# Dense V tiles loaded in pairs: two buffers of two tiles in place of four buffers of one

## The chip, the cores and the metric

The kernel runs on one core of a Trainium2 chip. The metric is the device time of one execution in microseconds (us), the median of several executions. Trace times count from the first instruction of one profiled execution.

## What is computed

One layer of a hybrid backbone for 256 tokens of width 2048: a long-convolution branch and a state-space branch, merged and projected, and then a retrieval of experts (PEER). Only the last step of the retrieval matters here. For each token there are 128 chosen experts (8 heads, 16 each) out of 16,384, and their rows of `peer_v` (2048 wide) are added up with weights:

```python
def block(args):
    hb, ib, gb = args
    act = jax.nn.gelu(jnp.einsum('td,tkd->tk', hb, p['peer_u'][ib]))
    return jnp.einsum('tk,tkd->td', act * gb, p['peer_v'][ib])
```

After it comes the last layer norm of `alpha * h + gate * ffn`, and the output.

## The kernel before

`block_ef` holds the end of the kernel. The sum over `peer_v` is done in two ways at once, one for each half of the 2048 columns.

**Columns 0 to 1023, dense, on TensorE.** All 16,384 rows of `peer_v` are read as 128 tiles (`v_dense[i]`, 128 experts x 1024 columns, float32, 512 KB, 4 KB for each partition). The weights were spread out beforehand into matrices `W[t][...]` (most of them zero) by one-hot products, which keep DVE and TensorE at work until the sums can begin. `sum_tile(i)` (L2716 to L2726) waits for tile i and multiplies it for both token tiles t and both column halves k into the four PSUM banks `2 * t + k`, where all 128 tiles are added up. The trace has two matmul records for each of these float32 products, eight for a tile. The last product of a tile raises `vt_used`.

**The buffers.** `v_tile` (L1968) is `m.yhy`, cut into four slots of 1024 columns. The two rows `h2` of modulated tokens, which the dot products with `peer_u` read, lie in the same memory: row 0 in slots 0 and 1, row 1 in slots 2 and 3. So tiles 0 and 1 wait until the first half of those dot products is done, and tiles 2 and 3 until all are. From tile 4 on, the load of tile i waits for `vt_used` to reach i - 3, that is, until tile i - 4 has been multiplied. SP (SyncE) issues them in order (L2122 to L2129), and nothing else goes through SP meanwhile; after them come the four stores of the output.

**Columns 1024 to 2047, gathered, on GpSimd and DVE.** For each of the 2 x 128 pairs (token tile, chosen expert), GpSimd issues a gather (L2165) of 128 rows of 1024 columns, again 512 KB in rows of 4 KB, and DVE adds it, times a coefficient, to `acc` (`add_row`, L2498; the first two are L2495). Eight slots hold gathered rows: four in `scores`, four in `m.h`. GpSimd waits with gather k until the row that was in its slot has been added. The last 24 gathers (from `V_LATE` = 232) use only the four slots of `scores`, because `m.h` is loaded again with the residual rows (ACT, L2303) once 232 rows are added.

**The end.** When all 256 rows are added, DVE finishes the late columns (`finish_late_columns`, L2506 to L2513), then reads the four PSUM banks of the dense sums (`finish_early_columns`, from L2521; it waits for `ffn_pe`), normalises, and SP stores the output. DVE reads the banks in the order in which TensorE's last tile finishes them.

So two chains run side by side, and both draw on the same 16 DMA engines: load, multiply, release of a `v_tile` slot (SP, TensorE); and gather, add, release of a row slot (GpSimd, DVE).

Of the kernel before, what the change touches and what calls it, by code (L numbers as in the profile page):

```python
# [41 lines left out]
PH, NKEY, TOPK = 8, 128, 16  # L42
# [1852 lines left out]
def block_ef(nc, m, d):  # L1895
# [4 lines left out]
    with ExitStack() as ctx:  # L1900
# [3 lines left out]
        def sem(name):  # L1904
            return ctx.enter_context(nc.semaphore(name))
# [62 lines left out]
        v_tile = m.yhy[:].rearrange("p a b -> p (a b)").rearrange("p (s n) -> p s n", n=HALF_D)  # L1968
        NVT = 4
# [50 lines left out]
        w_a = sem("expert_weights_copied")  # L2020
        v_in = [sem(f"v_row_{n}_gathered") for n in range(NV)]
        acc_v = sem("v_rows_added")
        vt_in = [sem(f"v_tile_{n}_loaded") for n in range(NVT)]
        vt_used = sem("v_tiles_done")
        ffn_pe = sem("ffn_summed")
        gt2_in = sem("last_gate_row_loaded")
# [14 lines left out]
        def dve_rows(j):  # L2041

            return j + 1 - min((j + 1) // 4, N_PE)
# [50 lines left out]
        with nc.Block() as block:  # L2094

            @block.sync
            def _(sp):
                for dst, src in ((sc2, d.mod_rows[2 * KT:3 * KT]), (sh2, d.mod_rows[KT:2 * KT])):
                    sp.dma_start(dst.rearrange("p (o n) -> p o n", o=1),
                                 src.rearrange("(o a) n -> o (a n)", o=1).unsqueeze(0).to_broadcast([P, 1, D])).then_inc(mods_in, 16)  # L2100
                sp.dma_start(iota[:], d.iota).then_inc(small, 16)

                def store_h(t):
                    sp.wait_ge(h_fin, t + 1)
                    sp.dma_start(d.h_rows[:, t, :], m.h[:, t, :]).then_inc(h_st[t], 16)

                for n in range(RING + OUT_EARLY, N_OUT + SQ_TILES - N_HOME):
                    sp.wait_ge(m.w_used, START_OUT + n - RING + 1)
                    src = d.w_out[OUT_ORDER[n]] if n < N_OUT else d.w_q[n - N_OUT + (N_HOME if n >= N_OUT + 4 else 0)]
                    sp.dma_start(m.ring[:, n % RING, :], src).then_inc(m.w_full[n % RING], 16)  # L2110
                    if n == 26:
                        store_h(0)
                    if n == N_OUT:
                        sp.dma_start(keys[:].rearrange("p a b -> p (a b)"), d.keys.rearrange("p a b c -> p (a b c)")).then_inc(keys_in, 16)
                    if n == N_OUT + 3:
                        for k, home in enumerate(homes):
                            if k == 2:
                                store_h(1)
                                sp.wait_ge(h2_p, 2 * TT + 1)
                            sp.dma_start(home, d.w_q[4 + k]).then_inc(home_in[k], 16)  # L2120

                for i in range(NKEY):  # L2122
                    if i == 0:
                        sp.wait_ge(dot_v, dve_rows(ROWS // 2 - 1))
                    if i == 2:
                        sp.wait_ge(dot_v, N_DVE)
                    if i >= NVT:
                        sp.wait_ge(vt_used, i - NVT + 1)
                    sp.dma_start(v_tile[:, i % NVT, :], d.v_dense[i]).then_inc(vt_in[i % NVT], 16)  # L2129

                for k in range(2 * TT):
                    sp.wait_ge(out_v, k + 1)
                    t, part = k // 2, slice(k % 2 * HALF_D, (k % 2 + 1) * HALF_D)
                    sp.dma_start(d.out[t * P:(t + 1) * P, part], m.h[:, t, part]).then_inc(out_st, 16)
                sp.wait_ge(out_st, 16 * 2 * TT)
# [174 lines left out]
            def _(v):  # L2310
# [177 lines left out]
                def add_row(k):  # L2488

                    t, first = k % TT, k < TT  # L2490
                    _, landed = v_before(k)
                    coefficient = gate[:, v_pair(k):v_pair(k) + 1]
                    v.wait_ge(v_in[v_at(k)], landed)
                    if first:
                        nc.vector.tensor_scalar(acc[:, t, :], v_slot[v_at(k)], coefficient, None, ALU.mult).then_inc(acc_v, 1)  # L2495
                    else:
                        v.wait_ge(acc_v, k - 1)
                        nc.vector.scalar_tensor_tensor(acc[:, t, :], v_slot[v_at(k)], coefficient, acc[:, t, :],  # L2498
                                                       ALU.mult, ALU.add).then_inc(acc_v, 1)
# [93 lines left out]
            def _(pe):  # L2593
# [121 lines left out]

                def sum_tile(i):  # L2716

                    pe.wait_ge(vt_in[i % NVT], 16 * (i // NVT) + 16)
                    for t in range(TT):
                        for k in range(2):  # L2720
                            mm = nc.tensor.matmul(ps[:, 2 * t + k, :], W[t][i // HALF][:, i % HALF, :], v_tile[:, i % NVT, k * CH:(k + 1) * CH],
                                                  start=(i == 0), stop=(i == NKEY - 1))
                            if i == NKEY - 1:
                                mm.then_inc(ffn_pe, 1)
                    if i < NKEY - 1:
                        mm.then_inc(vt_used, 1)  # L2726
# [19 lines left out]
                for u in range(UNITS):  # L2746
                    for h in range(NB):
                        k = NB * u + h
# [18 lines left out]
                for i in range(NKEY):  # L2767
                    sum_tile(i)
# [16 lines left out]
def build(nc, d):  # L2785
    with ExitStack() as ctx:
# [36 lines left out]
        m.b_in = ctx.enter_context(nc.semaphore("e_bias_row_loaded"))  # L2823
        block_d(nc, m, d)
        block_ef(nc, m, d)


# [116 lines left out]
```

## Time and profile before

| | us |
|---|---|
| median of 3 runs (3486.7 to 3492.4) | 3490.19 |
| the profiled execution | 3493.18 |
| its span, first to last instruction | 3491.5 |
| first and last record of a dense sum, TensorE | 2966.4, 3405.6 |
| last addition of a gathered row begins, DVE | 3459.65 |
| DVE begins to read the dense sums | 3468.26 |

The times in the rows are read as positions in the span: the first eight tenths of it do other work, the stretch from 2966 to 3461 is the two chains, and the last 30 us are the finish. PE is TensorE, PEld its weight loads, DVE is VectorE, POOL is GpSimd and SP is SyncE. DMA queue q0 carries the gathers that GpSimd issues, q1 what SP issues (in this stretch the dense tiles alone), q10 what ACT issues. A packet of this stretch is one row of 4 KB, so a dense tile is 128 packets, to which 16 small ones are added that report its end: 144.

### The profile page before, as it was taken

How to read it: one execution, taken by the hardware profiler on the slowest of the kernel's cores; microseconds unless marked ns; L12 is line 12 of the kernel's file. 1: busy time of each engine (PE TensorE's matmuls, PEld its weight loads, DVE VectorE, ACT ScalarE, POOL GpSimd, SP SyncE). 2: the span in 40 equal slices, each digit the busy share in tenths (PEclk: the TensorE clock that was granted, in tenths of full speed). 3: DMA queues.
4: the chain of work that ended last, by engine and by line, in shares of the span. 5: the costliest groups of instructions: out<-in, count | busy, mean ns of one | idle time of the engine just before them, and what ended most of it. 6: DMA issues, size and time to landing. Idle time of an engine off the chain costs nothing. (4 is left out here: it accounts for less than half of the span.)

```text
span 3491.5 us, 35993 instructions
## 1 busy us (share of the span) xinstructions
PE 3175.9 (91%) x12602; PEld 2031.3 (58%) x12602; DVE 2136.3 (61%) x3994; ACT 635.7 (18%) x1127; POOL 996.9 (29%) x618
## 2 busy tenths in 40 slices
PE   7999999999999999999999999887677768999990
PEld 2456667575757666777544444666666766444440
DVE  6543444444434444665756425888899988666667
ACT  2312212121212122111000011233233424000000
POOL 0011102020211113000000011455644462876773
PEclk8999999999999999999999999998888889999995
DMA  9754454545364544554554597999998893999996
GB/s 359 291 219 181 181 200 166 216 152 224 129 234 154 209 183 182 202 186 174 206 180 169 211 334 281 384 374 377 394 385 337 318 396 152 394 419 420 419 419 245
DMA packets 171354, 930.26 MB, mean 266 GB/s; under 512 B 19736, under 2 KB 32857, under 8 KB 89305
## 3 DMA queue, kind: packets, MB, share of 16 engines
q1 hardware_dynamic: 85386, 494.13, 38.0%
q0 software_dynamic: 73728, 402.69, 28.9%
q10 hardware_dynamic: 12112, 31.79, 2.3%
q8 instruction: 74, 1.21, 0.1%
q14 instruction: 54, 0.44, 0.0%
HBM read 907.29 MB, written 21.23 MB: 266 GB/s over the span
## 5 line engine op out<-in xcount | busy, mean ns | idle before, releaser
L1078 PE MATMUL ps<-mT,ring 128*128 128x256 f32 (+1 forms) x4096 | 1168.9, 446 | 1.1 <-PEq L215 1.1
L1078 PEld LDWEIGHTS ps<-mT,ring 128*128 128x128 f32 x4096 | 774.9, 190 | 388.1 <-issue 318.3
L2156 POOL DMA_INDIRECT u_rows<-in_peer_u_dram,expert_indices x172 | 267.9, 1558 | 283.9 <-DVE dots L2453 117.0
L2453 DVE CUSTOM_DVE_ANT_0 u_rows<-u_rows,yhy 128x2048 f32<-128x2048 f32 x130 | 293.8, 2287 | 57.8 <-DMA u_rows<-in_peer_u_dram,expert_indices 44.6
L2669 PE MATMUL ps<-mT,turned_rows 128*128 128x128 f32 x2016 | 301.0, 304 | 22.3 <-ACT turned_rows L2230 20.7
L2669 PEld LDWEIGHTS ps<-mT,turned_rows 128*128 128x128 f32 x2016 | 279.1, 216 | 38.0 <-issue 38.0
L710 POOL TENSOR_TENSOR dd<-mask_f,dt_g 128x1024 f32<-128x1024 f32 x16 | 30.4, 1897 | 933.1 <-DVE dt_g L980 932.4
L2165 POOL DMA_INDIRECT scores<-in_v_rest_dram,expert_indices x140 | 203.1, 1451 | 136.0 <-DVE turned_rows L2495 56.2
L870 DVE SCALAR_TENSOR_TENSOR conv<-ps,tap_g,conv 128x510 f32<-128x510 f32 (+1 forms) x48 | 33.8, 704 | 338.7 <-ACT conv L731 338.7
L2498 DVE SCALAR_TENSOR_TENSOR turned_rows<-scores,expert_gate,turned_rows 128x1024 f32<-128x1024 f32 x138 | 176.9, 1286 | 96.8 <-DMA scores<-in_v_rest_dram,expert_indices 95.8
L2230 ACT COPY turned_rows<-ps 128x512 f32<-128x512 f32 x252 | 144.1, 586 | 439.7 <-PE ps L2661 433.6
L2661 PE MATMUL ps<-ident,u_rows 128*128 128x128 f32 x672 | 117.2, 318 | 84.6 <-DMA u_rows<-in_peer_u_dram,expert_indices 84.6
L2498 DVE SCALAR_TENSOR_TENSOR turned_rows<-h_rows,expert_gate,turned_rows 128x1024 f32<-128x1024 f32 x116 | 148.7, 1286 | 72.7 <-DMA h_rows<-in_v_rest_dram,expert_indices 72.6
L2165 POOL DMA_INDIRECT h_rows<-in_v_rest_dram,expert_indices x116 | 166.2, 1433 | 57.0 <-issue 29.3
L2156 POOL DMA_INDIRECT h_rows<-in_peer_u_dram,expert_indices x84 | 133.4, 1588 | 116.2 <-DVE dots L2453 55.3
L2453 DVE CUSTOM_DVE_ANT_0 h_rows<-h_rows,yhy 128x2048 f32<-128x2048 f32 x63 | 142.9, 2287 | 29.2 <-DMA h_rows<-in_peer_u_dram,expert_indices 22.6
L884 DVE SCALAR_TENSOR_TENSOR ada_sums<-ada_tiles,csil,ada_sums 128x1024 f32<-128x1024 f32 x120 | 153.9, 1283 | 4.0
L2661 PEld LDWEIGHTS ps<-ident,u_rows 128*128 128x128 f32 x672 | 94.8, 166 | 96.7 <-DMA u_rows<-in_peer_u_dram,expert_indices 93.5
L870 DVE SCALAR_TENSOR_TENSOR hyb<-ps,tap_g,hyb 128x255 f32<-128x255 f32 x48 | 23.1, 480 | 199.0 <-ACT hyb L731 199.0
L1245 PE MATMUL ps<-ring,mT 128*128 128x256 f32 x512 | 129.1, 386 | 0.3 <-PEq L645 0.3
L731 ACT ACTIVATE conv<-ps,tap_g 128x512 f32<-128x512 f32 (+1 forms) x48 | 35.5, 742 | 510.2 <-PE ps L1078 509.1
L2713 PE MATMUL ps<-keys 128*128 128x128 f32 x512 | 105.5, 335 | 21.9 <-DVE keys L2477 19.8
(392 smaller groups left out, 4475.2 us busy)
## 6 DMA issues: line engine op xcount, KB each, us to landing
ring<-in_w_stream_dram SPq DMA_DIRECT2D x160, 1024.0 KB, 4.9
ada_tiles<-in_w_ada_dram SPq DMA_DIRECT2D x64, 1024.0 KB, 6.7
yhy<-in_v_dense_dram SPq DMA_DIRECT2D x128, 512.0 KB
ring<-in_w_mix_dram SPq DMA_DIRECT2D x48, 1024.0 KB, 4.8
ring<-in_w_mod_dram SPq DMA_DIRECT2D x32, 1024.0 KB, 10.5
ring<-in_w_out_dram SPq DMA_DIRECT2D x32, 1024.0 KB, 7.3
rows<-cum_rows_scratch SPq DMA_DIRECT2D x16, 1536.0 KB, 13.0
ring<-in_w_q_dram SPq DMA_DIRECT2D x12, 1024.0 KB, 9.4
```

What stands on the lines that cost most here:

```text
L870: nc.vector.scalar_tensor_tensor(view[:, :, 1:T], src[:, :, 0:T - 1], tap[:, ci, 0:1], view[:, :, 1:T], ALU.mult, ALU.add).then_inc(conv_v, 1)
L884: nc.vector.scalar_tensor_tensor(adas[:], adat[:, b, j, :], m.csil[:, k, 0:1], adas[:], ALU.mult, ALU.add).then_inc(ada_used, 1)
L1078: mm = nc.tensor.matmul(ps[:, k % 4, 0:n], m.ring[:, slot, kt * P:(kt + 1) * P], m.mT[:, kt, 0:n], start=(kt == 0), stop=(kt == KT - 1))
L1245: mm = nc.tensor.matmul(gate_region(m, j), a, w, start=(i == 0 and kk == 0 and j == 6), stop=(i == 3 and kk == 1 and j in (1, 3, 5, 6)))
L2156: nc.gpsimd.indirect_dma_start(u_slot[j % NU], None, d.peer_u, bass.IndirectOffsetOnAxis(ap=eidx[:, j:j + 1], axis=0)).then_inc(u_in[j % N ...
L2165: nc.gpsimd.indirect_dma_start(v_slot[v_at(k)], None, d.v_rest, bass.IndirectOffsetOnAxis(ap=eidx[:, v_pair(k):v_pair(k) + 1], axis=0)).th ...
L2230: nc.scalar.copy(turned_rows[:, g, :], ps[:, g % 2, :]).then_inc(turn_a, 1)
L2453: nc.vector.tensor_tensor_reduce(out=u_slot[j % NU], in0=u_slot[j % NU], in1=h2[:, t, :], scale=1.0, scalar=0.0, op0=ALU.mult, op1=ALU.add ...
L2498: nc.vector.scalar_tensor_tensor(acc[:, t, :], v_slot[v_at(k)], coefficient, acc[:, t, :], ALU.mult, ALU.add).then_inc(acc_v, 1)
L2661: mm = nc.tensor.transpose(ps[:, g % 2, a * P:(a + 1) * P], row[:, i * P:(i + 1) * P], m.ident[:])
L2669: mm = nc.tensor.matmul(ps[:, 2 + k % 2, 0:P], turned_rows[:, g, a * P:(a + 1) * P], m.mT[:, i, T + t * P:T + (t + 1) * P], start=(i == 0) ...
L2713: mm = nc.tensor.matmul(ps[:, 4 + k % 4, a * NKEY:(a + 1) * NKEY], one_hot[:, s, :], one_hot[:, s + 1, :], start=True, stop=True)
```

## The change

Two tiles are loaded by one DMA of 1 MB. Pair k (tiles 2k and 2k + 1) goes to slots 0 and 1 if k is even, and 2 and 3 if it is odd. `sum_tile` is the same apart from its wait: both tiles of a pair wait for the pair's semaphore, so the first tile waits until both have landed. A pair's load waits until both tiles of pair k - 2 have been multiplied. The memory used is the same.

```diff
-        vt_in = [sem(f"v_tile_{n}_loaded") for n in range(NVT)]
+        vt_in = [sem(f"v_tile_pair_{n}_loaded") for n in range(2)]
...
-                for i in range(NKEY):
-                    if i == 0:
+                for k in range(NKEY // 2):
+                    if k == 0:
                         sp.wait_ge(dot_v, dve_rows(ROWS // 2 - 1))
-                    if i == 2:
+                    if k == 1:
                         sp.wait_ge(dot_v, N_DVE)
-                    if i >= NVT:
-                        sp.wait_ge(vt_used, i - NVT + 1)
-                    sp.dma_start(v_tile[:, i % NVT, :], d.v_dense[i]).then_inc(vt_in[i % NVT], 16)
+                    if k >= 2:
+                        sp.wait_ge(vt_used, 2 * (k - 1))
+                    sp.dma_start(v_tile[:, 2 * (k % 2):2 * (k % 2) + 2, :],
+                                 d.v_dense[2 * k:2 * k + 2].rearrange("a p n -> p a n")).then_inc(vt_in[k % 2], 16)
...
-                    pe.wait_ge(vt_in[i % NVT], 16 * (i // NVT) + 16)
+                    pe.wait_ge(vt_in[i // 2 % 2], 16 * (i // NVT) + 16)
```

The order of the instructions on SP, from the last load before the dense tiles to the end. `yhy` is the memory of `v_tile`. The semaphores have names of earlier stages, whose numbers are used again. Before:

```order
L2110 DMA ring<-in_w_q_dram 128x2048 [waits ring_tiles_used] x8
L2129 DMA yhy<-in_v_dense_dram 128x1024 [waits filter_abs_summed]
L2129 DMA yhy<-in_v_dense_dram 128x1024
L2129 DMA yhy<-in_v_dense_dram 128x1024 [waits filter_abs_summed]
L2129 DMA yhy<-in_v_dense_dram 128x1024
L2129 DMA yhy<-in_v_dense_dram 128x1024 [waits b_dve_step] x124
L2134 DMA out_dram<-h_rows 128x1024 [waits ada_tile_0_loaded] x4
```

and now:

```order
L2110 DMA ring<-in_w_q_dram 128x2048 [waits ring_tiles_used] x8
L2129 DMA yhy<-in_v_dense_dram 128x2x1024 [waits filter_abs_summed] x2
L2129 DMA yhy<-in_v_dense_dram 128x2x1024 [waits small_loaded] x62
L2135 DMA out_dram<-h_rows 128x1024 [waits ada_tile_0_loaded] x4
```

128 loads become 64 of twice the size. The first two have the waits that tiles 0 and 2 had, and the other 62 wait for the products, `vt_used`.

On TensorE, four of the last tiles. A row with a wait is the first product of a tile, and the semaphore it names is that of the tile's load. Before:

```order
L2721 MATMUL ps<-yhy,ring 128x512 [waits x_loaded]
L2721 MATMUL ps<-yhy,ring 128x512
L2721 MATMUL ps<-yhy,mT 128x512 x2
L2721 MATMUL ps<-yhy,ring 128x512 [waits dft_matrix_loaded]
L2721 MATMUL ps<-yhy,ring 128x512
L2721 MATMUL ps<-yhy,mT 128x512 x2
L2721 MATMUL ps<-yhy,ring 128x512 [waits small_loaded]
L2721 MATMUL ps<-yhy,ring 128x512
L2721 MATMUL ps<-yhy,mT 128x512 x2
L2721 MATMUL ps<-yhy,ring 128x512 [waits first_small_loaded]
```

and now:

```order
L2722 MATMUL ps<-yhy,ring 128x512 [waits x_loaded]
L2722 MATMUL ps<-yhy,ring 128x512
L2722 MATMUL ps<-yhy,mT 128x512 x2
L2722 MATMUL ps<-yhy,ring 128x512 [waits x_loaded]
L2722 MATMUL ps<-yhy,ring 128x512
L2722 MATMUL ps<-yhy,mT 128x512 x2
L2722 MATMUL ps<-yhy,ring 128x512 [waits dft_matrix_loaded]
L2722 MATMUL ps<-yhy,ring 128x512
L2722 MATMUL ps<-yhy,mT 128x512 x2
L2722 MATMUL ps<-yhy,ring 128x512 [waits dft_matrix_loaded]
```

No product has moved. Four semaphores in turn have become two, each waited for by two tiles in a row, of which the second finds it raised already.

## Rows read from the trace of the kernel before

**Rows 1.** By stage: busy us (instructions) of PE, PEld, DVE, ACT, POOL; clock, DMA share, GB/s

```profile
2950.00:3000.00 50.00, 48.41 (x146) 24.92 (x147) 37.37 (x85) 9.52 (x19) 28.60 (x18) 1.00 0.59 234
3200.00:3250.00 50.00, 50.00 (x118) 22.23 (x117) 32.84 (x26) 0.00 (x0) 36.46 (x26) 1.00 1.03 420
3350.00:3400.00 50.00, 50.00 (x117) 22.04 (x116) 32.58 (x27) 0.00 (x0) 37.48 (x26) 1.00 1.03 420
3400.00:3450.00 50.00, 6.17 (x15) 2.47 (x13) 36.12 (x29) 0.00 (x0) 28.50 (x27) 0.59 0.90 332
```

**Rows 2.** The dense sums' line L2721: duration ns min/median/max, first and last start

```profile
L2721 PE MATMUL ps<-yhy,gates x256: 592/592/697, 2966.4 to 3184.1; 128*128 128x512 f32 x128
L2721 PE MATMUL ps<-yhy,mT x256: 592/592/593, 3188.0 to 3405.6; 128*128 128x512 f32 x128
```

**Rows 3.** DVE at the end, in order of time: start us, us

```profile
3459.65 1.28 DVE L2498 SCALAR_TENSOR_TENSOR turned_rows<-scores,expert_gate,turned_rows 128x1024 f32<-128x1024 f32 x1 [1.13 <-DMA scores<-in_v_rest_dram,expert_indices]
...
3468.26 0.69 DVE L2521 TENSOR_TENSOR turned_rows<-keys,ps 128x512 f32<-128x512 f32 x1
```

**Rows 4.** Additions of gathered rows (L2498) alone, by stretch

```profile
3000.00:3400.00 400.00, 260.26 (x203) 1.00 1.03 420
3400.00:3414.00 14.00, 13.07 (x11) 0.81 1.02 414
3414.00:3461.00 47.00, 30.73 (x25) 0.50 0.80 279
```

**Rows 5.** GpSimd's gathers (L2165): duration ns min/median/max, first and last start

```profile
L2165 POOL DMA_INDIRECT scores<-in_v_rest_dram,expert_indices x136: 934/1491/7846, 2966.2 to 3454.2; - x136
```

**Rows 6.** SP's issues of dense tiles, in order of time

```profile
2970.17 0.33 SPq L2129 DMA_DIRECT2D yhy<-in_v_dense_dram  x1
...
3196.77 0.33 SPq L2129 DMA_DIRECT2D yhy<-in_v_dense_dram  x1
...
3392.47 0.33 SPq L2129 DMA_DIRECT2D yhy<-in_v_dense_dram  x1
```

**Rows 7.** DMA queues from 3395.15 to 3395.85: packets, MB, share of 16 engines

```profile
q0 software_dynamic: 79, 0.28, 98.8%
q8 instruction: 1, 0.02, 8.5%
```

**Rows 8.** DMA queues from 3199.30 to 3199.95, then from 3199.95 to 3202.60

```profile
q0 software_dynamic: 73, 0.27, 101.5%
q1 hardware_dynamic: 5, 0.00, 0.4%
...
q0 software_dynamic: 161, 0.59, 54.0%
q1 hardware_dynamic: 131, 0.52, 48.1%
```

**Rows 9.** Loads of 1 MB on q1 beside gathers of peer_u: L2110 from 2213 to 2272

```profile
L2110 SPq DMA_DIRECT2D ring<-in_w_q_dram x4: 328/328/328, 2213.5 to 2271.4; - x4
...
DMA to landing us min/median/max: 8.7/9.4/10.2
```

**Rows 10.** DMA queues from 2971.1 to 2973.5, where no gather moves

```profile
DMA packets 144, 0.52 MB, mean 218 GB/s; under 512 B 16, under 2 KB 16, under 8 KB 144
...
q1 hardware_dynamic: 144, 0.52, 62.8%
```

**Rows 11.** Short stretches with idle time on TensorE, each with the next one

```profile
2395.00:2398.40 3.40, 1.23 (x9) 1.03 (x10) 3.40 (x5) 0.87 (x2) 3.09 (x2) 1.00 0.99 371
2398.40:2401.80 3.40, 3.40 (x17) 3.40 (x18) 0.14 (x2) 0.79 (x2) 2.61 (x3) 0.50 1.05 388
...
2077.60:2081.00 3.40, 2.24 (x14) 1.35 (x12) 2.07 (x3) 2.16 (x7) 0.00 (x0) 1.00 0.99 265
2081.00:2084.40 3.40, 2.66 (x10) 1.45 (x10) 0.00 (x0) 3.40 (x11) 1.80 (x1) 1.00 1.01 429
```

## Prediction, before the changed kernel was run

> **What bounds the kernel now.** I read first the busy time by stage, then who waits at the end. From 3000 to 3400 two things are full: TensorE is busy 50 of every 50 us, and the DMA engines move 420 GB/s [rows 1]. After 3400 TensorE is done (its last record starts at 3405.6 [rows 2]), and what is left are gathered rows: the last addition begins at 3459.65, and DVE turns to the dense sums at 3468.26 [rows 3]. So the gathers set the end and the dense sums have slack: 3468.3 less some 3406 is 62 us, and a little more, since DVE reads four banks one after the other.
>
> TensorE's pace is (3405.6 - 2966.4) / 128 = 3.43 us for a tile [rows 2], so the dense tiles draw 0.524 MB / 3.43 us = 153 GB/s. The gathers take what is left, 267 GB/s: 203 rows in 400 us, 1.97 us for a row [rows 4]. An addition takes 1.28 us (260.26 / 203) and GpSimd can issue a gather in 0.93 us [rows 4, 5], so neither of them is the limit; the shared DMA bandwidth is. **Each byte that the dense tiles do not draw goes to the gathers.** That is why a slower TensorE need not be a loss here, up to the 62 us.
>
> **How long a load takes.** The question is whether a pair lands in time. Now: the last tile is issued at 3392.47 [rows 6], and up to 3395.85 no packet of q1 moves [rows 7]: it starts 3.4 us after its issue. In mid-stretch the tile issued at 3196.77 [rows 6] moves between 3199.95 and 3202.60, 0.52 MB in at most 2.65 us, with 161 gather packets beside its own 131 [rows 8]: the two queues share about evenly, and the start is 3.2 us behind the issue. With 0.5 us until the report is seen (my estimate, no row shows it), a tile lands 6.5 us after its issue. It has three tiles of time, 10.3 less 0.3 for the release, so 3.5 us are to spare; TensorE's full busy time agrees.
>
> **The change, part by part.** (1) *64 issues fewer on SP.* SP does nothing else, 0.33 us each [rows 6], hidden: nothing. The 16 small packets of each saved load are too short to count: five took 0.4% of the engines in 0.65 us [rows 8]. (2) *First pairs.* Pairs 0 and 1 have the waits of tiles 0 and 2 and land before 2966 as they did: nothing. (3) *The second tile's wait* finds its semaphore raised: nothing. (4) *The pair's load.* It is issued when pair k - 2 is done and needed when pair k - 1 is: 6.87 us later, less 0.3. It moves twice the bytes. Its start is not shown for a DMA of this shape; I keep 3.4 us. Two packets for one of before, at the same even share, take 4.7 to 5.1 us; with 0.5 us at the end it lands **9.0 us** after its issue. Lower bound: if it moved alone at 420 GB/s, 2.5 us, it would land at 6.4 and TensorE would not wait. Upper bound: loads of the same 1 MB on the same queue beside gathers took 8.7 to 10.2 us, median 9.4 [rows 9]. I take 9.0, by the packets, near that median.
>
> (5) *What TensorE waits.* With two buffers, pair k ends no earlier than pair k - 2 ends + 0.3 + 9.0 + 0.05 + 6.87 = 16.2 us later: two pairs in 16.2 us where it was 13.74. That is a wait of 2.4 us for every two pairs, in one piece or in two of 1.2; on average a pair takes **8.1 us** instead of 6.87. As first order, 62 pairs x 1.2 = 75 us, over the slack of 62. Two things change it.
>
> (6) *The gathers gain.* The dense draw falls to 1.05 MB / 8.1 = 130 GB/s, and the gathers get 290: 1.81 us for a row, 0.16 less. About 220 rows fall into this: 35 us. The 232nd row, added at about 3414 now (25 additions are in the last stretch, which starts at 3414 [rows 4]), comes at about 3380. The last 24 rows have four slots and take 47 us [rows 4]; now dense loads run beside them, so I give them 47 to 60, take 54, and the gathers end near 3434, 27 us earlier. TensorE by then has done 2 pairs (to 2980) and 454 / 8.1 = 56 more; the 6 that are left no longer share the bandwidth (a tile without gathers moved at 218 GB/s within 3.3 us of its issue [rows 6, 10], so 1 MB in 4.8 us and about 6 in all is in time) and take 41 us. TensorE ends at about 3475 instead of 3407.
>
> (7) *The end.* DVE's finish from the first read of a bank is 3491.5 - 3468.3 = 23.2 us [rows 3]; it can start 2.6 us before TensorE's end. 3475 + 20.6 = **3496**, 4 us above the span of before: the gathers' gain is spent, and TensorE ends last.
>
> (8) *The clock.* Where TensorE was busy 1.23 of 3.4 us, the next 3.4 us have a granted clock of 0.50, the lower level of 1.2 GHz; where it was busy 2.24 of 3.4 it stayed at 1.00 [rows 11]. A wait of 2.4 us in one piece leaves TensorE some 1.0 of 3.4 us, as in the first case; one of 1.2 us leaves 2.2, as in the second. A stretch at half clock costs 1.7 us of products. Between none of some 28 double periods (0) and two thirds of them (32 us), I take a third, 16 us. It is on the path now, since TensorE ends last. Sum: 3496 + 16 = 3512 of span; the executions lie 1.7 above the span in the profiled one, whose time is 3.0 above the median, so 1.3 less than that span: **3511**.
>
> **A rule weighed.** A tile issued at 2970.17, when no gather moves, is over by 2973.5, at 218 GB/s [rows 6, 10]; beside gathers it takes 6.5 us. The Trainium skill, "DMA: Bandwidth & Descriptors", section "Bandwidth", asks for DMAs of at least 1 MiB, and in "Anatomy of one DMA" prices one at 2.0 us plus its bytes at 436 GB/s. By that, an estimate for the pair is 4.4 us, inside the 6.6 that it has; the 6.5 us for half as much beside gathers disagree with it, and I go by the trace. It would make rival A true.
>
> **Rivals.**
> *A. Nothing waits* (the pair is in time, or the change only halves the number of issues). The draw is the same, and so is the time: 3490. It needs a landing within 6.6 us, which a single tile takes already beside gathers. It speaks for it that the tile has 3.5 us to spare; against it that the pair has 3.4 us less time and 2.4 us more to move.
> *B. TensorE waits, but less than its slack: faster.* Landing near 8 us: (8.0 + 7.2) / 2 = 7.6 us for a pair, a draw of 138 GB/s, 282 for the gathers, 0.1 us less for each of 220 rows, 24 us earlier at row 232, of which the last 24 rows give back some 10; TensorE ends near 3450 and the gathers set the end: 14 us off, 3476. It would follow if a pair moved in 3.8 us, two packets of its own for one of the gathers'. The skill's same page, "Queues, rings and completion order", says that an engine drains a whole packet of descriptors (9 to 17) of one queue before it turns to the next, which would favour the longer load so. Against it, the even mix through a tile's 2.6 us [rows 8]. The turn from faster to slower is at a landing of about 8.8 us without any loss of clock.
> *C. TensorE waits for more and the clock falls often: slower by more.* The forecast's own mechanism; its far end is a landing of 9.6 or more (start or movement longer for a DMA with two rows for each partition) and two thirds of the waits at half clock: (9.6 + 7.2) / 2 = 8.4 us, TensorE near 3488 + 32, 3541 of span.
> *D. The total bandwidth changes* because the packets of a pair alternate between two tiles 512 KB apart. 1% of 420 GB/s over 430 us is 4 us either way; no row shows it.
>
> **Chances.** Landing over 8.8 us and TensorE last, the forecast with its far end: 0.64 slower. Around the turning point (0.11) or rival A (0.05): 0.16 within. Rival B: 0.20. A measurement of this kernel tells about 0.2% (7 us) from no change, which is the bound of these three. The range takes in B and most of C, 3476 to 3540.
>
> **What the new profile would show.** TensorE's waits for the dense loads: 60 to 75 us in total, as pieces of up to 2.4 us (A: none; B: 30 to 45). The last record of the dense sums near 3480 to 3500, behind the last gathered row, which should be near 3425 to 3440. In mid-stretch DVE adds a row every 1.8 us, and q1 shows runs of 256 packets over about 5 us, starting 3.4 us after the issue. Granted clocks below 1.00 between 2980 and 3440. If the gathers still end last, B or A holds; if the pair's landing is below 8, step 4 is wrong; if TensorE waits as said and the clock stays at 1.00, step 8 is.

## The result: 0.8% slower, and TensorE ends last

The changed kernel takes 3515.6 us (median; 3511.6 to 3526.4) where the kernel before takes 3489.3 in the same comparison: a ratio of 1.008, 95% interval 1.0056 to 1.0104. 3511 was forecast, with 3476 to 3540 as the range.

The profiled execution is the longest of its four, 3526.4 us with a span of 3524.7, 11 us over the median. Terms read from its trace are therefore a little large; a second profile of the same kernel, below, lies at the median. In all the profiles of this document the first dense product starts between 2962.0 and 2968.5 us, though no edit changes the work ahead of it. Where two profiles differ by a few us, the lengths of the chains say more than the times at which they end.

The stages, columns as in [rows 1]:

```profile
3100.00:3150.00 50.00, 44.26 (x101) 18.57 (x101) 36.02 (x29) 0.00 (x0) 30.18 (x29) 1.00 1.03 420
3200.00:3250.00 50.00, 43.49 (x96) 18.20 (x94) 35.37 (x29) 0.00 (x0) 31.22 (x29) 0.97 1.03 420
3350.00:3400.00 50.00, 39.31 (x77) 16.74 (x78) 31.61 (x25) 0.00 (x0) 24.34 (x22) 0.86 0.99 400
3450.00:3500.00 50.00, 50.00 (x118) 22.09 (x117) 0.00 (x0) 0.00 (x0) 0.00 (x0) 1.00 0.41 147
```

TensorE is no longer full between 3000 and 3400: in the second row it is busy 43.5 of 50 us and finishes only 96 records, where it was 118. The DMA engines still move 420 GB/s up to 3350. After 3450 no gathered row is left to add, and TensorE works on alone.

The dense sums (line L2722 now), against [rows 2] (duration in ns, lowest, median and highest; then the first and last start):

```profile
L2722 PE MATMUL ps<-yhy,gates x256: 592/592/1222, 2968.5 to 3239.0; 128*128 128x512 f32 x128
L2722 PE MATMUL ps<-yhy,mT x256: 592/592/1061, 3242.9 to 3503.4; 128*128 128x512 f32 x128
```

They take 535 us instead of 439, and some products take twice their time (up to 1222 ns). What TensorE's products waited for, in total us, number of waits and longest:

```profile
PE ps L2722 <- DMA yhy<-in_v_dense_dram: 62.8, 30, 6.4
```

One of these waits, in square brackets in the order of time, and the records behind it:

```profile
3234.21 1.98 PE L2722 MATMUL ps<-yhy,gates 128*128 128x512 f32 x4 [2.73 <-DMA yhy<-in_v_dense_dram]
3236.03 1.88 PE L2722 MATMUL ps<-yhy,u_rows 128*128 128x512 f32 x4
```

The landings of the 44 pairs issued from 2990 to 3370, one every 8.56 us (a landing is the time from the issue until the semaphore is raised):

```profile
L2129 SPq DMA_DIRECT2D yhy<-in_v_dense_dram x44: 367/368/368, 2999.2 to 3367.3; - x44
...
DMA to landing us min/median/max: 8.7/8.9/10.2
```

One pair as an example. Its issue on SP, and then the DMA queues from 3231.6 to 3234.9 and from 3234.9 to 3240.35 (packets, MB, share of the 16 engines):

```profile
3231.51 0.37 SPq L2129 DMA_DIRECT2D yhy<-in_v_dense_dram  x1
```

```profile
q0 software_dynamic: 305, 1.10, 81.3%
q1 hardware_dynamic: 85, 0.28, 21.1%
...
q0 software_dynamic: 337, 1.24, 55.6%
q1 hardware_dynamic: 272, 1.05, 46.8%
```

All its 272 packets (256 of 4 KB and 16 small ones) lie in the second stretch, more than 3.4 us behind the issue; the 85 of the first stretch belong to the pair before. It moves at an even share with the gathers, the same mix as in [rows 8]. Its rows take 5.1 of the 5.4 us, the rest is for the small packets. Over the 44 pairs the medians, taken from the packets of the trace, are: the first packet 3.5 us after the issue (3.3 to 3.55), the rows moved in 5.0 us (4.7 to 6.2), the landing 0.5 us behind them.

The gathered rows, against [rows 4]: the additions by stretch, the last of them, and DVE's first read of a dense sum. A wait is in square brackets:

```profile
3000.00:3350.00 350.00, 250.23 (x198) 0.95 1.03 420
3378.00:3435.00 57.00, 31.69 (x25) 0.91 0.92 347
```

```profile
3433.66 1.28 DVE L2499 SCALAR_TENSOR_TENSOR turned_rows<-scores,expert_gate,turned_rows 128x1024 f32<-128x1024 f32 x1 [2.63 <-DMA scores<-in_v_rest_dram,expert_indices]
...
3501.50 0.69 DVE L2522 TENSOR_TENSOR turned_rows<-keys,ps 128x512 f32<-128x512 f32 x1 [59.25 <-PE ps L2722]
```

A row takes 1.77 us where it took 1.97, and the last is added 26 us sooner than in [rows 3]. But DVE, which had no wait for the dense sums before, now waits 59.25 us for TensorE.

### The profile page after: what moved, and what is told of

The parts are those of the page before. It is cut to its first block and busy times, and to the rows that moved or that the text cites. A ratio compares the mean times of both kernels' runs of the same rounds, so it can differ in the third digit from the quotient of the medians.

```text
span 3524.7 us, 35929 instructions
## 1 busy us (share of the span) xinstructions
PE 3206.1 (91%) x12602; PEld 2036.3 (58%) x12602; DVE 2134.0 (61%) x3994; ACT 635.1 (18%) x1127; POOL 913.5 (26%) x618
## 5 line engine op out<-in xcount | busy, mean ns | idle before, releaser
L2166 POOL DMA_INDIRECT scores<-in_v_rest_dram,expert_indices x140 | 166.6, 1190 | 166.3 <-DVE turned_rows L2499 78.2
L2722 PE MATMUL ps<-yhy,gates 128*128 128x512 f32 x256 | 132.5, 643 | 35.4 <-DMA yhy<-in_v_dense_dram 34.2
L2722 PE MATMUL ps<-yhy,ring 128*128 128x512 f32 x256 | 130.5, 635 | 28.7 <-DMA yhy<-in_v_dense_dram 28.6
L2166 POOL DMA_INDIRECT h_rows<-in_v_rest_dram,expert_indices x116 | 128.5, 1108 | 69.7 <-DVE turned_rows L2499 41.2
```

Of the source, the lines that this page charges most:

```text
L2166: nc.gpsimd.indirect_dma_start(v_slot[v_at(k)], None, d.v_rest, bass.IndirectOffsetOnAxis(ap=eidx[:, v_pair(k):v_pair(k) + 1], axis=0)).th ...
```

## Experiments

### The changed kernel again

No edit, in another comparison.

> The changed kernel again, unedited, beside the others of this call. Theory: the waits for pairs come from the landing time and are there in each execution, 3508 to 3524; how often the granted clock falls to 0.50 in the stretch of the dense sums differs from one execution to the next, and with it the time by some us.

Measured: 3516.05 us (3514.7 to 3520.9), ratio 1.0082, interval 1.0064 to 1.0099. Its profiled execution took 3514.7. What its products waited for:

```profile
PE ps L2722 <- DMA yhy<-in_v_dense_dram: 61.3, 32, 4.0
```

The waits are those of the first profile (62.8 us in 30); its span is 11.7 us shorter. The stretch from 2980 to 3440 in the two, first profile above, this one below:

```profile
2980.00:3440.00 460.00, 396.97 (x850) 166.83 (x849) 319.48 (x253) 1.28 (x1) 272.53 (x244) 0.94 1.01 410
```

```profile
2980.00:3440.00 460.00, 400.08 (x872) 168.31 (x871) 319.40 (x255) 1.28 (x1) 271.20 (x241) 0.96 1.02 412
```

If the granted clock is either 1.00 or 0.50, a mean of 0.94 means that 0.12 of the 460 us, 55 us, were at 0.50; here it is 37 us. While the products run, each of these us costs half a us, so the first profile lost 9 us more to the clock. That is not the whole of the 11.7 us between the two spans: the dense sums began at 2968.5 in the first and at 2964.4 in the second, so 4.1 us arose ahead of them, and the sums themselves took 534.9 and 527.3 us, 7.6 apart.

### What the pair costs: coarse release, or the wait for both tiles

The change does two things at once. A slot is released later, with its neighbour, and the first tile of a pair waits for the second one's bytes. To part them, the kernel before gets two loads of one tile each, issued together at the pair's release; each tile keeps its own semaphore.

```diff
-                    if i >= NVT:
-                        sp.wait_ge(vt_used, i - NVT + 1)
+                    if i >= NVT and i % 2 == 0:
+                        sp.wait_ge(vt_used, i - NVT + 2)
```

> The kernel before with one edit: the loads of tiles i and i + 1 (i even) are issued together, when both tiles of the pair two back are multiplied. Each tile keeps its own DMA, semaphore and slot, so the release is as coarse as in the change and the wait is not. Theory (TensorE waits because the first tile of a pair is held until 1 MB has landed, 8.9 us after the issue, where 6.6 us are to be had): the first tile lands 6.5 us after its issue and is needed at 6.6, the second lands near 9 and is needed near 10. TensorE waits 0 to 20 us in total, the dense sums end at 3410 to 3430, time 3480 to 3492. Rival (the coarse release, which leaves two tiles of prefetch, is what costs): as the changed kernel, waits near 150 us, time 3510 to 3520.

Measured: 3493.9 us (3490.0 to 3500.7) against 3491.9, ratio 1.0007, interval 0.9997 to 1.0017: no change that can be told. The waits of TensorE's products:

```profile
PE ps L2721 <- DMA yhy<-in_v_dense_dram: 5.8, 8, 1.1
```

The release is as coarse as in the change and as little is prefetched, 1 MB. What is gone is the wait of the first tile for the second one's bytes. The time is 2 us over the upper end that was expected.

Next, the same two loads, but on one semaphore, and TensorE waits for both:

```diff
...
-                    sp.dma_start(v_tile[:, i % NVT, :], d.v_dense[i]).then_inc(vt_in[i % NVT], 16)
+                    sp.dma_start(v_tile[:, i % NVT, :], d.v_dense[i]).then_inc(vt_in[i // 2 % 2], 16)
...
-                    pe.wait_ge(vt_in[i % NVT], 16 * (i // NVT) + 16)
+                    pe.wait_ge(vt_in[i // 2 % 2], 32 * (i // NVT) + 32)
```

> As e1_two_loads, but both loads of a pair raise one semaphore, and TensorE waits until both have landed, as in the change. Only the shape of the DMA differs from the changed kernel: two of 512 KB in a row in place of one of 1 MB. Theory (the wait for the whole pair costs, the DMA's shape does not): as the changed kernel, 3508 to 3522, landing of the second tile 8.6 to 9.0 us after the first issue. Rival (a DMA of two rows for each partition is slow or starts late by itself): clearly under 3500.

Measured: 3523.8 us (3521.2 to 3526.4), ratio 1.0098, interval 1.0078 to 1.0117, 2 us over the upper end that was expected. The waits:

```profile
PE ps L2721 <- DMA yhy<-in_v_dense_dram: 64.4, 29, 4.9
```

One edit, the shared semaphore, takes the waits from 5.8 to 64.4 us and the time from 3493.9 to 3523.8. The shape of the DMA is not to blame: with two DMAs of 512 KB it is at least as slow as with one of 1 MB, 1.0098 against 1.0080 and 1.0082, with intervals that overlap.

### Three slots of one tile

The kernel before, with three slots for single tiles instead of four.

```diff
-        NVT = 4
+        NVT = 3
```

> The kernel before with three slots of one tile in place of four, so that a load has two tiles of time less the release, 6.6 us, as in the change, but only 512 KB to move. Theory (what decides is landing against window, and a single tile lands at 6.5): TensorE just keeps up, with short waits where a tile lands late, 5 to 25 us in total, dense sums end at 3412 to 3430, time 3482 to 3492. Rival (prefetch depth in bytes decides; 1 MB ahead, as much as in the change): waits of 75 us or more, over 3500.

Measured: 3493.2 us against 3490.2, ratio 1.0011, interval 1.0001 to 1.0020; 1 us over the upper end expected. The landings in mid-stretch, and TensorE's waits:

```profile
DMA to landing us min/median/max: 6.3/6.5/7.6
```

```profile
PE ps L2721 <- DMA yhy<-in_v_dense_dram: 6.6, 12, 0.9
```

The window is the time from the issue of a load until TensorE needs it. It is the same as the pair has, 6.6 us. A tile that lands in 6.5 us costs 6.6 us of waits in it, and the pair, which lands in 8.9, costs 63. So what decides is the landing against the window, and not the bytes that are loaded ahead, which are 1 MB in both.

### The pair without the gathers

The changed kernel without gathers 8 to 255 and their additions, and so without most of the sum of the late columns.

> The changed kernel without gathers 8 to 255 and their additions (most of the late columns' sum is left out), so that pairs are loaded with the DMA engines to themselves. Theory (the pair is late because it starts 3.5 us after its issue and shares the bandwidth): it starts 1 us after its issue, lands within 6.3 us, TensorE never waits in the dense sums, which end 440 us after they begin, near 3408, at a clock of 1.00; time near 3430. Rival (a DMA of this shape takes 8 us or more by itself): waits as in the change, near 3500.

Measured: 3437.2 us (one execution), where near 3430 was expected. Landings from 2965 to 3420, and TensorE's waits:

```profile
DMA to landing us min/median/max: 4.7/4.8/13.3
```

```profile
PE ps L2722 <- DMA yhy<-in_v_dense_dram: 6.5, 1, 6.5
```

From 3000 to 3400 TensorE is busy throughout:

```profile
3000.00:3400.00 400.00, 400.00 (x934) 177.10 (x933) 0.00 (x0) 0.00 (x0) 0.00 (x0) 1.00 0.44 152
```

A DMA of 1 MB with two rows for each partition lands in 4.8 us when no gather moves, and in 8.9 beside the gathers. The expectation had no wait at all. The single one ends at 2986.6, behind the load of the residual rows, which this kernel issues at 2973.0.

### The clock

The changed kernel with one extra product behind each pair, into a bank that nobody reads:

```diff
                     if i < NKEY - 1:
                         mm.then_inc(vt_used, 1)
+                    if i % 2 and i < NKEY - 1:
+                        nc.tensor.matmul(ps[:, 5, :], m.ident[:], gate_rows[:, 0, 0:CH], start=True, stop=True)
```

> The changed kernel with one more product (128x512, into a bank that nobody reads any more, 0.86 us) behind each pair on TensorE, after the pair's release. It adds 0.86 us of work for each pair where the loads leave 1.2 to 1.4 us of waiting. Theory (some 15 stretches of 3.4 us at a granted clock of 0.50 are on the path, 1.7 us each): the waits shrink by what the fillers take, the clock stays at 1.00 between 2980 and 3440, the dense sums end some 20 us sooner, near 3483, time 3492 to 3502. Rival 1 (the half-clock stretches fall into time that TensorE would wait anyway): no change, 3510 to 3520. Rival 2 (the fillers lie on the path): later by up to 62 x 0.86 = 53 us.

Measured: 3512.5 us (3511.2 to 3512.9), ratio 1.0061, interval 1.0042 to 1.0080. The stretch and the waits:

```profile
2980.00:3440.00 460.00, 441.00 (x1007) 187.85 (x1007) 314.78 (x249) 0.00 (x0) 273.97 (x243) 1.00 1.02 414
```

```profile
PE ps L2722 <- DMA yhy<-in_v_dense_dram: 20.1, 30, 2.9
```

The clock stays at 1.00. The 63 products of 0.86 us (54 us) fill most of what was waiting (61 to 63 us, now 20), and the time is 3 us under the changed kernel's, not 20. It was measured beside another set of executions of the kernel before; by the ratios, 1.0061 against 1.0082, it is 7 us, with intervals that overlap. I had not counted that the last pairs, issued after the gathers, wait for next to nothing, so that the product is on the path there. So it was left out behind the last ten:

```diff
-                    if i % 2 and i < NKEY - 1:
+                    if i % 2 and i < 108:
```

> As e2_filler, but with the extra product only behind the first 54 pairs, which share the DMA engines with the gathers; the last pairs, which wait for nothing, have none. Theory (the half-clock stretches cost about 20 us in the profiled execution of the change, of which the fillers of the last pairs gave some 8 back in e2_filler): no half-clock stretch, dense sums end near 3482, time 3500 to 3507. Rival (the clock costs nothing in the median execution): as the changed kernel, 3511 to 3518.

Measured: 3507.4 us (3506.5 to 3508.3), against 3516.05 (3514.7 to 3520.9) for the changed kernel in the same comparison; the two sets do not overlap. It is 0.4 us over the upper end expected. More products make the kernel 8.7 us faster. In its stretch from 2980 to 3440 the mean clock was 0.99, and the waits:

```profile
PE ps L2722 <- DMA yhy<-in_v_dense_dram: 21.1, 30, 4.3
```

The 8.7 us are the least that the clock cost, since the extra products take time too. An estimate of the whole from the traces, against the second profile of the change: here 54 products add 46.4 us, the waits are 40.2 shorter, and the dense sums take 519.8 us instead of 527.3. So the products of the sums themselves ran some 14 us faster. With the 63 products (54.2 us more work, waits 41.2 shorter, sums 4.3 shorter), where the clock never fell, it is 17 us. The mean clock gave 18.

### The residual rows' load

Once 232 rows are added, ACT loads 2 MB of residual rows. In the change it does so at 3379, while pairs and gathers still share the DMA engines; TensorE's longest wait, 6.4 us, follows (4.0 us in the second profile). Here the residual rows are loaded after the last gathered row.

```diff
-                act.wait_ge(acc_v, V_LATE)
+                act.wait_ge(acc_v, ROWS)
                 act.dma_start(m.h[:], d.h_rows).then_inc(h_in, 16)
-                act.wait_ge(acc_v, ROWS)
```

> The changed kernel with one edit: the 2 MB of residual rows are loaded on ACT's queue after the last gathered row and not 24 rows before. In the change this load begins at 3379 and lands 10.8 us later, and the pair that is under way then keeps TensorE waiting 6.4 us. Theory (TensorE ends last, so that wait is on the path, and the later load is hidden behind the dense sums): the wait of 6.4 us shrinks to about 2, time 4 to 6 us under the changed kernel's. Rival (it is made up elsewhere): no difference.

Measured: 3516.9 us against 3516.05, ratio to before 1.0084. The waits:

```profile
PE ps L2721 <- DMA yhy<-in_v_dense_dram: 65.0, 32, 3.0
```

The long wait is down to 1.9 us, as expected, but neither the total nor the time is smaller. The trace shows where the waits went:

```profile
3427.11 1.99 PE L2721 MATMUL ps<-yhy,ring 128*128 128x512 f32 x4 [2.88 <-DMA yhy<-in_v_dense_dram]
3444.14 1.98 PE L2721 MATMUL ps<-yhy,ring 128*128 128x512 f32 x4 [3.03 <-DMA yhy<-in_v_dense_dram]
```

From 3375 to 3450 the waits are 11.6 us here and 8.0 in the second profile of the change. The one that ends at 3444.1 follows the late load, which is issued at 3428.7: moving the load moved its wait with it. Why the pairs before it wait for more than in the change stays open.

### Is a slower TensorE free up to the slack?

The prediction's rival B needs this. In the kernel before, the load of tile i now waits for the first product of tile i - 2 in place of the last of tile i - 4. That is one tile and one product later, 3.43 + 0.86 = 4.3 us; the 7.7 us of the expectation count a tile too many.

```diff
...
-                        sp.wait_ge(vt_used, i - NVT + 1)
+                        sp.wait_ge(vt_used, i - 1)
...
-                    if i < NKEY - 1:
-                        mm.then_inc(vt_used, 1)
+                            elif t == 0 and k == 0:
+                                mm.then_inc(vt_used, 1)
```

> The kernel before with one edit: the load of tile i waits for the first product of tile i - 2 instead of the last of tile i - 4, and so is issued some 7.7 us later, at a fixed 0.9 us after the end of tile i - 3. Four slots and single tiles stay. Theory (what TensorE's dense loads do not draw goes to the gathers, and up to about 60 us of delay on TensorE is free): a tile takes (0.3 + 6.5 + 0.9 + 3.43 + 3.43 - 3.43) / 3 = 3.7 us, the dense sums end near 3440, the gathers draw 278 GB/s, 1.89 us for a row, and end 12 to 18 us sooner, near 3445; time 3470 to 3480, faster than before. Rival (the gathers do not gain, since GpSimd or DVE limits them): gathers end at 3460, time 3490. Rival 2 (waits of 0.3 us for each tile lower the clock): dense sums end over 3480, time over 3500.

Measured: 3487.3 us (3477.2 to 3493.6) against 3491.9, ratio 0.9986, interval 0.9974 to 0.9997, where 3470 to 3480 was expected. The last records of the dense sums and of the additions, and the additions from 3000 to 3370:

```profile
L2721 PE MATMUL ps<-yhy,mT x256: 592/592/593, 3217.4 to 3466.0; 128*128 128x512 f32 x128
L2498 DVE SCALAR_TENSOR_TENSOR turned_rows<-scores,expert_gate,turned_rows x138: 1273/1285/1335, 2963.0 to 3446.7; 128x1024 f32<-128x1024 f32 x138
```

```profile
3000.00:3370.00 370.00, 257.56 (x202) 1.00 1.03 420
```

The gathers gain, 1.83 us for a row. Their end is 13 us sooner, of which 3 lie ahead of the stage, whose additions began at 2963.0 and not at 2966.0. TensorE ended 26 us later than I expected: with the wait on tile i - 2, its cycle is 0.9 + 0.3 + 6.5 us for two tiles, 3.85 for each (3.93 in the trace), and not the 3.7 of my sum, which went over three. So DVE waited 8.8 us for TensorE, and most of the gain was gone. The full delay was then kept to the first 100 tiles; from there on a load waits for the first product of tile i - 3:

```diff
-                        sp.wait_ge(vt_used, i - 1)
+                        sp.wait_ge(vt_used, i - 1 if i < 100 else i - 2)
```

> As e5_balanced (single tiles, four slots, loads issued later), but only for tiles 4 to 99; from tile 100 on a load is issued after the first product of tile i - 3, so that it has the slack to stand the load of the residual rows and to end early. In e5_balanced a tile took 3.9 us and TensorE's end, 3466, was behind that of the gathers, 3448. Theory (the gain of the gathers is real, and the time is set by the later of the two chains): dense sums end near 3450, gathers at 3448 to 3452, time 3478 to 3484, 0.2 to 0.4% under before. Rival (the gathers give the gain back at the end): 3487 to 3492.

Measured: 3487.1 us (3482.3 to 3493.4) against 3491.6, ratio 0.9987, interval 0.9978 to 0.9996. The last dense record was at 3451.4 and the last addition at 3452.4, both about where expected, but the time is 3 us above what was. From the last addition to the end the span takes 31.8 us, as it did before (3491.5 - 3459.7), and the expected time left too little for that. Last, the gathers keep eight slots for eight rows more:

```diff
-        V_LATE = ROWS - 24
+        V_LATE = ROWS - 16
```

> As e10_balanced_early, and the gathers use all eight slots up to row 240 instead of 232, after which the residual rows are loaded. Before, the last 24 rows took 47 us at 279 GB/s, half of the DMA engines' idle time in this stage. Theory: the gathers end 3 to 6 us sooner than in e10_balanced_early, time 2 to 6 us under it, TensorE's end permitting. Rival (TensorE ends last there): no difference.

Measured: 3483.2 us (3480.2 to 3485.0), ratio 0.9974, interval 0.9963 to 0.9986. Its last records:

```profile
L2721 PE MATMUL ps<-yhy,mT x256: 592/592/593, 3214.3 to 3448.6; 128*128 128x512 f32 x128
L2498 DVE SCALAR_TENSOR_TENSOR turned_rows<-scores,expert_gate,turned_rows x134: 1270/1285/1350, 2962.1 to 3447.3; 128x1024 f32<-128x1024 f32 x134
```

Both chains end 3 to 5 us sooner than in the version before it, but in this profile both also began 2.6 us sooner. By its length the chain of the gathers gained 2.5 us and TensorE's nothing. The time is 4 us lower, as expected, though the executions of the two versions overlap. This kernel is faster than both of the case, by 8 us than the one before; how much of it `V_LATE` would give by itself was not tried.

## Why the prediction was right

**Landing (4).** Forecast 9.0 us, and measured 8.9 as the median, 8.7 to 10.2. The terms are right one by one: 3.5 us to the first packet for a forecast of 3.4, 5.0 of movement for 4.7 to 5.1, and 0.5 for the report, for which the prediction had only an estimate. The row that stood nearest, the 1 MB loads of another stage [rows 9], had the same ends.

**Waits (5).** 60 to 75 us in pieces of up to 2.4 were forecast; 62.8 in 30 pieces, 2.1 each on average, came, and 61.3 in 32. Eight pieces of the first profile were 2.5 to 2.9 us and one was 6.4; in the second seven were 2.6 to 3.1 and one 4.0. A pair took 8.5 us where step 5 had 8.1, because the products at half clock lengthen it too, which step 5 left out. That landing against window is the cause, and not the DMA's shape or the prefetched bytes, is shown by the experiments with two loads, with one semaphore, and with three slots. That the landing is long because of the gathers is shown by the kernel without them.

**Gathers (6).** 1.81 us for a row, row 232 at 3380 and an end near 3434 were forecast. The trace has 1.77 us, row 232 at 3377.8 and the last addition at 3433.7. A row is the 0.04 us faster because of the pair's 8.5 us: 1.05 MB / 8.5 = 123 GB/s leave 297 for the gathers, not 290. What TensorE did not draw did go to the gathers, as forecast, and did not help, since TensorE ended last.

**TensorE's end (6 to 8).** 3475 plus 16 for the clock, 3491, was forecast; the last record is at 3503.4 in the first profile and at 3491.7 in the second, whose time is near the median:

```profile
L2722 PE MATMUL ps<-yhy,mT x256: 592/592/1061, 3236.5 to 3491.7; 128*128 128x512 f32 x128
```

In length, the better measure, the forecast was 3491 - 2966.4 = 525 us; 527.3 came in the second profile and 534.9 in the first. Over the 439.2 of before these are 88 and 96 us. The waits make 61 and 63 of them and the clock 18 and 27, by its mean. The rest, 9 and 6 us, is about what a restart costs: four records last 1.88 us and begin 1.72 apart, and the four behind a wait last 1.98, which is 0.26 us for each of some 30 waits. From TensorE's last record to the end there are 21.3 us in both profiles, 20.6 forecast. No large error hides behind another here.

**The clock (8).** A third of the double periods was to cost 1.7 us each, 16 us. Here is one of the waits with the stretch behind it, columns as in [rows 11]:

```profile
3161.50:3164.90 3.40, 0.87 (x3) 0.45 (x3) 2.28 (x3) 0.00 (x0) 2.92 (x2) 1.00 1.03 419
3164.90:3168.30 3.40, 3.40 (x6) 1.34 (x5) 2.53 (x3) 0.00 (x0) 2.48 (x4) 0.50 1.02 420
```

The mechanism is as forecast: the granted clock falls to 0.50, the lower of its two levels, behind a stretch with a long wait, and the products in it take twice their time. The size: 27 us in the first profile and 18 in the second by the mean clock, at least 9 by the experiment with extra products and 14 to 17 by its traces. The second profile is near the median, so the forecast of 16 was near. But the third was a choice between none and two thirds, for which no row stood, and executions differ by as much as 9 us in it. That it came so near is luck.

**What was missing.** Of the load of the residual rows (2 MB) I said nothing as a cost to TensorE. It keeps one pair back by 6.4 us in the first profile; moving it behind the last gathered row gave no time.

**The rule weighed.** The price of a DMA that the prediction took from the Trainium skill, "DMA: Bandwidth & Descriptors", "Anatomy of one DMA", 4.4 us for the pair, is given there for DMAs that GpSimd issues, and the pair's is issued by SyncE. Without gathers the pair landed in 4.8 us, near that price; beside them in 8.9, twice as much. The prediction was right to go by the trace.

**The rivals.** A (nothing waits) falls with the landing of 8.9 us. B (TensorE waits less than its slack: faster) did not occur, but its mechanism is real: with single tiles and delayed loads, the two experiments at 0.9986 and 0.9987, with intervals that end below 1. It gave a third of the 14 us that B had, and with eight rows more in eight slots, 8 us. Longer bursts taking a larger share of the engines, B's condition, is refuted for this shape: 337 gather packets beside 272 of the pair. C's far end, a landing of 9.6 us, did not come, though the first profile lost nearly as much to the clock as C has (27 us against 32). D (another total bandwidth) falls with the 420 GB/s, the same as before.

## What to carry to other kernels

Merging loads into larger ones at the same memory makes the first piece wait for the last byte and shortens the time in which a load may land, here from three tiles of work to two, 10.0 to 6.6 us. Before doing so, take the landing time from the trace beside the traffic that will really run with it, and compare it with the work of one buffer; what a lone load takes (4.8 us here, against 8.9) says too little. And where two streams share full DMA engines, the one that is not last can be slowed down, but only up to the point where it becomes last.

## What was not expected

A load on q1 starts 1.0 us after its issue when no gather moves, and some 3.5 us after it beside gathers (medians of 3.4 to 3.5 for tiles and for pairs). In the kernel without gathers a pair is issued at 3201.80; no packet moves up to 3202.75, and all of them do between 3202.75 and 3206.40. Its issue, and the packets of the two stretches:

```profile
3201.80 0.37 SPq L2129 DMA_DIRECT2D yhy<-in_v_dense_dram  x1
```

```profile
DMA packets 0, 0.00 MB, mean 0 GB/s; under 512 B 0, under 2 KB 0, under 8 KB 0
```

```profile
DMA packets 272, 1.05 MB, mean 287 GB/s; under 512 B 16, under 2 KB 16, under 8 KB 272
```

Beside gathers with rows of 8 KB the late start is the same as beside those of 4 KB. In the kernel before, a load of 1 MB is issued at 2236.20, and the DMA queues from 2236.19 to 2239.49 show the gathers alone:

```profile
q0 software_dynamic: 193, 1.42, 101.6%
```

So the start does not depend on the size of the gathers' rows, as far as these two show, nor on whether the load has 128 or 256 packets. Of the 4.1 us that the gathers add to a pair's landing, some 2.5 are the later start, and only some 1.6 are the shared bandwidth (the rows move in 5.0 us beside gathers and in 3.4 without). Why gathers put the start off was not tried. The 287 GB/s of the lone pair are also more than the 218 of a lone tile in [rows 10], from which I had worked out 6 us for its landing. And more products on TensorE made the kernel faster by 8.7 us, since they kept the granted clock up, at 0.99 on average.
